# Gate and up matrices of a mixture of experts tiled by input chunks, with a wait and a release for each half

## The reference

```python
def expert_choice_ffn(h, w_router, w_gate, w_up, w_down):
    b, n, d = h.shape
    cap = max(1, (EC_CAPACITY * n) // N_EXPERTS)
    aff = jax.nn.softmax((h @ w_router).astype(jnp.float32), axis=-1)
    g, idx = lax.top_k(jnp.swapaxes(aff, 1, 2), cap)
    xe = jax.vmap(lambda hb, ib: hb[ib])(h, idx)
    a = jnp.einsum('becd,edf->becf', xe, w_gate)
    up = jnp.einsum('becd,edf->becf', xe, w_up)
    y = jnp.einsum('becf,efd->becd', jax.nn.silu(a) * up, w_down) * g[..., None].astype(h.dtype)
    return jax.vmap(lambda ib, yb: jnp.zeros((n, d), h.dtype).at[ib.reshape(-1)].add(yb.reshape(-1, d)))(idx, y)
```

## Time and profile before

| | |
|---|---|
| median of 3 runs | 2900.12 us (2898.72 to 2900.56) |
| profiled execution, span from first to last instruction | 2896.6 us |
| PE busy | 2609.4 us (90%) |
| DVE busy | 1336.6 us (46%) |
| ACT busy | 961.9 us (33%) |
| POOL busy | 39.3 us (1%) |
| bytes moved | 796.13 MB, mean 275 GB/s |
| mean granted clock of PE | 0.968 of full |
| chain that ended last | PE 72%, DMA 19%, DVE 4%, ACT 3%, issue 2% |

### The profile page before, as it was taken

The page is one execution under the profiler, slowest core; times in us unless marked ns, Lnnn a source line. Parts: engine busy times, 40 slices in busy tenths (PEclk is TensorE's granted clock), DMA queues, the critical chain, the costliest instruction groups (busy, mean ns, idle before and its releaser), DMA issues.

```text
span 2896.6 us, 34037 instructions
## 1 busy us (share of the span) xinstructions
PE 2609.4 (90%) x13004; PEld 1714.1 (59%) x13004; DVE 1336.6 (46%) x2308; ACT 961.9 (33%) x1782; POOL 39.3 (1%) x51
## 2 busy tenths in 40 slices
PE   8999878787889888877779899999999999999999
PEld 3436423222465543222245789878988988985787
DVE  1764300001266520000025687567887458865676
ACT  3124210101121320000013555556555446544443
POOL 0010000000000000000000000000000000000000
PEclk9999999999999999999999999989999999999999
DMA  8674499999945459999991486515866427852242
GB/s 362 278 306 192 203 428 429 428 429 429 428 193 224 168 231 429 428 428 429 428 394 63 164 340 251 236 59 217 322 263 256 172 113 269 343 212 88 83 178 102
DMA packets 59492, 796.13 MB, mean 275 GB/s; under 512 B 8636, under 2 KB 9916, under 8 KB 10748
## 3 DMA queue, kind: packets, MB, share of 16 engines
q1 hardware_dynamic: 55664, 790.13, 66.8%
q10 hardware_dynamic: 3724, 4.59, 0.5%
HBM read 793.64 MB, written 1.05 MB: 274 GB/s over the span
## 4 chain that ended last, share of the span: by engine, by line
PE 72%; DMA 19%; DVE 4%; ACT 3%; issue 2%; SPq 0%; ACTq 0%; DVEq 0%; POOL 0%; POOLq 0%
PE banks L2008 12%; PE banks L2032 9%; PE banks L1504 8%; DMA ring<-in_t_gate 7%; PE banks L925 6%; DMA ring<-in_t_up 6%; PE banks L810 5%; PE banks L940 5%; DMA ring<-in_t_down 4%; PE banks L1520 3%; DMA arena<-in_t_gate 3%; PE banks L2025 2%; PE banks L1379 2%; PE banks L1573 2%; PE banks L797 2%
## 5 line engine op out<-in xcount | busy, mean ns | idle before, releaser
L1504 PE MATMUL banks<-ring,arena 128*64 128x512 f32 x1920 | 475.3, 619 | 100.9 <-DMA ring<-in_t_up 54.8
L1504 PEld LDWEIGHTS banks<-ring,arena 128*64 128x64 f32 x1920 | 162.3, 143 | 389.1 <-issue 345.4
L2633 DVE TENSOR_TENSOR arena<-arena,banks 128x512 f32<-128x512 f32 x32 | 22.0, 687 | 795.2 <-PE banks L1504 795.2
L3096 DVE TENSOR_TENSOR ring_lo<-ring,w_hi 128x1024 fp32r<-128x1024 f32 x256 | 313.3, 1225 | 133.9 <-ACT w_hi L2427 131.7
L2427 ACT CAST w_hi<-ring 128x1024 fp32r<-128x1024 f32 x256 | 268.4, 1055 | 314.9 <-PE banks L2008 166.3
L2032 PE MATMUL banks<-u_pair,w_hi 128*128 128x256 f32 x1536 | 278.8, 284 | 3.9 <-DVE ring_lo L3096 3.3
L2140 ACT COPY arena<-banks 32x512 f32 x96 | 55.3, 576 | 608.3 <-PE banks L1520 607.5
L2032 PEld LDWEIGHTS banks<-u_pair,w_hi 128*128 128x128 f32 x1536 | 240.1, 192 | 6.7 <-issue 3.9
L1520 PE MATMUL banks<-ring,arena 128*64 128x512 f32 x896 | 206.9, 616 | 28.4 <-DMA ring<-in_t_down 15.7
L2032 PE MATMUL banks<-u_pair,ring_lo 128*128 128x256 f32 x768 | 217.3, 283 | 0.0
L2008 PE MATMUL banks<-w_hi,ffn_h_hi 128*128 128x512 f32 x512 | 200.9, 392 | 0.0
(11 more groups left out here) (391 smaller groups left out, 4098.8 us busy)
## 6 DMA issues: line engine op xcount, KB each, us to landing
ring<-in_t_ffn SPq DMA_DIRECT2D x64, 2048.0 KB, 8.2
ring<-in_t_gate SPq DMA_DIRECT2D x60, 2048.0 KB, 22.0
ring<-in_t_up SPq DMA_DIRECT2D x60, 2048.0 KB, 22.1
ring<-in_t_down SPq DMA_DIRECT2D x56, 2048.0 KB, 21.6
ring<-in_t_ada_dots SPq DMA_DIRECT2D x48, 2048.0 KB, 9.7
ring<-in_t_ada SPq DMA_DIRECT2D x24, 2048.0 KB, 17.1
ring<-in_t_ret_in SPq DMA_DIRECT2D x12, 2048.0 KB, 8.2
arena<-in_t_down SPq DMA_DIRECT2D x8, 2048.0 KB, 31.3
```

The source lines that it names most:

```text
L1504: mm = nc.tensor.matmul(PS[64 * h:64 * h + 64, f.bank, :], x_cur[:, b, k, :], wview(un[h0 + h], KC)[:, k, :], start=(k == 0), stop=(k == K ...
L3096: TT(w_lo, w, w_hi[:, n % 4].bitcast(F32), ALU.subtract).then_inc(S("ffn_w_lo"), 1)
```

## The change

- `weight_tiles` cuts gate and up with `rows(m, 4)`, as down already is: unit h now holds input chunks 4h to 4h+3 and all 1024 output columns.
- In `plan_moe`, the first unit of each matrix has a `used` mark of its own, on the semaphore `moe_half`; the second keeps the bank's `full` mark. There are three such marks in an expert, 12 in a round, 48 in a mixture.
- In the expert loop PE waits for a unit right before the first chunk that reads it, and the last matmul of chunk 3 of each matrix raises `moe_half`.
- The `selT` transposes become the function `turn_selw(lo)`, two token tiles at a call, each with its own wait on `moe_selw`. With two sequences the first two tiles are turned inside the gather, after the first half (`k0 == 0`) of the second sequence, and the last two after the gather. With one sequence both are turned after the gather, where they stood.

```diff
@@ weight_tiles
-        "t_gate": experts(w["w_gate"], columns),
-        "t_up": experts(w["w_up"], columns),
+        "t_gate": experts(w["w_gate"], lambda m: rows(m, 4)),
+        "t_up": experts(w["w_up"], lambda m: rows(m, 4)),
@@ plan_moe
-                for i, f in enumerate((g, g, u, u, d, d)):
-                    us[6 * j + i].used = f.full
+                for i, f in enumerate((g, u, d)):
+                    us[6 * j + 2 * i].used = Mark(S("moe_half"), 48 * l + 3 * j + i + 1, 12)
+                    us[6 * j + 2 * i + 1].used = f.full
@@ moe_pe, before the gather
+                def turn_selw(lo):
+
+                    for t in range(lo, lo + TC):
+                        f = plan[p + "selT"][t]
+                        pe.wait_ge(S("moe_selw"), 4 * l + t + 1)
+                        f.open(pe)
+                        w = moe_selw[:, t].rearrange("p e c -> p (e c)")
+                        for q in range(4):
+                            mm = nc.tensor.transpose(PS[:, f.bank, q * P:(q + 1) * P], w[:, q * P:(q + 1) * P], ident)
+                        mm.then_inc(f.full.sem, 1)
@@ moe_pe, in the loop over k0 of the gather and behind it
-
-                pe.wait_ge(S("moe_selw"), (4 if l else 0) + 2 * ns)
-                for t, f in enumerate(plan[p + "selT"]):
-                    f.open(pe)
-                    w = moe_selw[:, t].rearrange("p e c -> p (e c)")
-                    for q in range(4):
-                        mm = nc.tensor.transpose(PS[:, f.bank, q * P:(q + 1) * P], w[:, q * P:(q + 1) * P], ident)
-                    mm.then_inc(f.full.sem, 1)
+                        if s == 1 and k0 == 0:
+                            turn_selw(0)
+
+                turn_selw(2 * ns - TC)
@@ moe_pe, gate and up
-                            un[h0].landed.wait(pe, it)
-                            un[h0 + 1].landed.wait(pe, it)
                             for k in range(KC):
+                                u = un[h0 + k // 4]
+                                if k % 4 == 0:
+                                    u.landed.wait(pe, it)
                                 for h in range(2):
                                     mm = nc.tensor.matmul(PS[64 * h:64 * h + 64, f.bank, :], x_cur[:, b, k, :],
-                                                          wview(un[h0 + h], KC)[:, k, :], start=(k == 0),
+                                                          wview(u, 4)[:, k % 4, h * 512:(h + 1) * 512], start=(k == 0),
                                                           stop=(k == KC - 1), skip_group_check=True)
+                                if k == 3:
+                                    mm.then_inc(S("moe_half"), 1)
                             mm.then_inc(f.full.sem, 1)
@@ moe_pe, down
-                        un[4].landed.wait(pe, it)
-                        un[5].landed.wait(pe, it)
                         ft.free.wait(pe, it)
                         for fc in range(8):
+                            if fc % 4 == 0:
+                                un[4 + fc // 4].landed.wait(pe, it)
                             for h in range(2):
...
+                            if fc == 3:
+                                mm.then_inc(S("moe_half"), 1)
                         mm.then_inc(fd.full.sem, 1)
```

## The result

The changed kernel takes 2884.45 us (median of 4 runs, 2884.28 to 2885.0) against 2900.28 us before: the ratio is 0.9949, with a 95% interval of 0.9935 to 0.9963. The profiled execution has a span of 2883.0 us against 2896.6.

The account below looks back on a forecast made before the run. Both mixtures were taken as bound by transfers, with 5.8 us of slack an expert. Gains of 8.7 and 7.1 us, 15.8 off a 2896.6 us span, gave 2880.8; plus 3.5 to the median, 2884.3 us, range 2880 to 2892.

Parts of the forecast that it names:

- The first release: Start of each mixture: gate's first unit is released after 4 of 8 chunks, so transfers start 3.55 us earlier.
- The stream doesn't pause: Both mixtures: transfers run without gaps from first issue to last landing, 4.897 us a unit, with 3.8 and 3.9 us remaining.
- The end: Last down of each mixture: only its second half follows the last landing, gaining 4.8 us in mixture 0, 3.55 in mixture 1.
- The transposes: Selection transposes before mixture 0's experts: moved into the gather, they let PE start 0.3 us sooner; mixture 1 unchanged.
- The added waits: Middle of each matrix in the expert loops: a wait already over costs 0, at most 0.1 us.
- The clock: PE in the mixtures: a fall costs it 1.43 to 1.69 us, taken by slack; waits become 1.35 us, twice as many.
- The second rival: Both mixtures: falls of PE's clock at the waits make PE the bound, +108 us less the 15.8, 2992; chance 0.03.
- The gain passes through: Behind the mixtures: `combine` and later work move along with down, so the whole gain reaches the total.
- its own bound of 2 us: Stages other than the mixtures: a change above 2 us in any would refute that the gain passes through.
- The sum: Whole kernel: 8.7 us from mixture 0 and 7.1 from mixture 1, together 15.8 us off the span, to 2880.8.

Follow-up runs that it names:

- the early release alone: The changed kernel, but PE waits for both units of a matrix at its start, measured against the kernel before: 2893.57 us, ratio 0.998.
- The transposes alone: The kernel before with only the selection transposes moved into the gather: 2898.45 us, ratio 0.9999.
- the split waits alone: The changed kernel, but both units of a matrix are released at its end, measured against the kernel before: 2892.19 us, ratio 0.9978.

## Why the prediction was right, step by step

**The first release.** Forecast 3.55 us in each mixture; measured 3.44 (7.13 - 3.69, and 7.12 - 3.69 in mixture 1). A half isn't half of 7.09 but 3.65 us: sixteen records more cost 3.44 us (7.09 - 3.65), and 0.21 us stand once in each group, however long. Otherwise right, and the early release alone shows that the start is handed on.

**The stream doesn't pause.** From first issue to last landing 439.2 us in mixture 0 (439.6 before) and 430.0 in mixture 1 (429.9). Right.

**The end.** Forecast 4.8 and 3.55 us; measured 8.39 - 3.65 = 4.7 and 7.09 - 3.66 = 3.4. The first half of down was to fit by 0.3 us in mixture 0 and by 0.2 in mixture 1; it fits by 0.20 and 0.06. Right, but narrowly, and with a share of luck: 1.3 of the 4.7 us are what the low clock in the last up cost the kernel before in this one profile. The transposes alone, with up and down of before, met none there. In the changed kernel the last up ran in two groups of 3.65 us, without low clock.

**The transposes.** Forecast 0.3, measured 0.5 to 0.6. Two terms were 0.1 off: ACT's last copy moved from 316.14 to 317.07, 0.93 us rather than 1.04, and PE starts 0.23 us after POOL's first copy (317.63 + 0.61, by the earlier trace rows), not 0.35. The 0.55 us in the first row of the table of stages would not show this by itself: in the profiles of kernels with the same code up to the loop of mixture 0 that start lies anywhere from 317.15 to 321.25 us.

**The added waits** cost nothing: 64 records in 13.95 us as before. That half matrices from one unit run as fast as from two: right.

**The clock.** The second rival wanted more falls. There are fewer: over four experts of mixture 1 the granted clock is 0.99 where the earlier trace rows had 0.96, with waits about half as long. The experiments separate the cause: over the two loops the granted clock is 0.96 and 0.96 in the kernel before, 0.95 and 0.96 with the early release alone, which still waits for whole matrices, but 1.00 and 0.99 with the split waits alone and in the changed kernel. So here it is the splitting of the waits that keeps the clock up, and not the early release. The stretch of four experts in the changed kernel:

```profile
1185.00:1302.00 117.00, 91.13 (x400) 28.59 (x398) 5.52 (x8) 8.28 (x13) 1.61 (x4) 0.99 1.01 429
```

The advice of the Trainium skill ("TensorE: Matmul & The Clock Gate", "HAM oscillation — how this bites in real kernels") to thin-M kernels, to run all K-tiles before waiting for a DMA, does not hold for this stage: the waits inside the K loop replace longer ones outside of it.

**The gain passes through.** Here a step failed by its own bound of 2 us: between the mixtures the changed kernel takes 2.16 us more. The stretches behind `combine` and ahead of the second loop carry it, in the changed kernel

```profile
765.05:795.58 30.53, 25.59 (x154) 19.41 (x153) 11.52 (x23) 10.48 (x17) 2.68 (x1) 0.94 1.01 426
...
983.99:1047.49 63.50, 52.14 (x226) 40.41 (x226) 23.01 (x59) 21.21 (x41) 1.18 (x3) 0.89 0.35 133
```

and in the kernel before

```profile
774.12:803.17 29.05, 24.09 (x153) 18.76 (x153) 11.52 (x23) 10.48 (x17) 2.68 (x1) 1.00 0.98 414
...
992.61:1054.40 61.79, 50.37 (x227) 39.97 (x226) 23.07 (x59) 21.20 (x41) 1.24 (x3) 0.92 0.36 137
```

The same work takes 1.48 and 1.71 us longer at a granted clock of 0.94 and 0.89 instead of 1.00 and 0.92; between the two stretches the changed kernel is 1.03 us faster (188.41 against 189.44). No part of the change can be named as the cause: the moved transposes alone have 282.57 us between the mixtures and the early release 282.52, but the split waits, with the same moved transposes, have 279.91. The changed kernel has 282.44 and 282.41 in its two profiles. So where a fall of the clock lands differs from kernel to kernel by up to 2.7 us here, and seems to stay with a kernel; what sets it is open, and a prediction made from one profile can't know it.

**The sum.** The mixtures and the transposes were forecast at 15.8 us and gave 15.8 (8.52 + 6.74 + 0.55). The span fell by only 13.6, for the reason just given. That the median came out at the forecast, 2884.45 for 2884.3, has some luck in it: I had taken 3.5 us between span and median for a constant. It is about 2.0 us of what lies around the span (2883.0 and 2885.0 in the changed kernel's profiled execution, the same in each experiment) and about 1.5 us by which the profiled execution of before was shorter than the median. The changed kernel's profiled execution was 0.55 us longer than its median (2885.0 against 2884.45). So the errors, 2.2 us lost on the way against 1.5 and 0.55 us of offset, nearly cancel.

## What to carry to other kernels

Where a stage is bound by a stream of transfers, its length is the time to the first release, the stream, and the work behind the last landing. Cut both ends by the order in which data are used, and check first, by count times pace against first issue to last landing, that nothing pauses between; then check that the finer pieces keep the pace, which here 2 MiB pieces did and 1 MiB pieces didn't. At the start, check the second and third release too: a first issue made 1.7 us sooner was worth nothing 95 us later, in the version in which the issue behind it came as late as before.

When a gain is under 1%, compare lengths of stages between marks in the profile, and not only medians: the parts of this change add up to within 0.4 us that way, beside runs that scatter by several microseconds.

## What the runs showed of the hardware

Splitting each 2 MiB transfer (16 KiB a partition) into two of 1 MiB took the stream from 428 to 422 GB/s, 1.5%. In the version that splits 4 of 24, 2.2 us were lost within the first 95 us of the loop, and 0.08 us for each split unit after that.

The largest difference between profiles came from the stick-breaking attention block, far from the change. In the profile of the early release alone the stretch from the end of its projections to its last heads took 53.5 us, in the changed kernel 60.7. The rows (columns as in the earlier trace rows) are of about the same work, first in the changed kernel, then in the early release alone:

```profile
1890.30:1920.00 29.70, 28.19 (x108) 21.30 (x108) 21.01 (x43) 15.52 (x29) 0.00 (x0) 0.71 0.36 142
...
1920.00:1951.00 31.00, 28.92 (x157) 21.81 (x156) 27.22 (x54) 21.15 (x42) 0.00 (x0) 1.00 0.00 1
```

```profile
1897.50:1925.00 27.50, 25.43 (x133) 19.58 (x134) 24.75 (x52) 19.42 (x37) 0.00 (x0) 1.00 0.39 154
```

At a granted clock of 0.71, more than half of the time at 1.2 GHz, the first stretch gets through 108 PE records in 29.7 us; at 1.00 it is 133 in 27.5. The low level lasts for some 17 us there: between 1900 and 1910 us the granted clock is 0.50 although PE is busy without a gap, and from 1910 to 1920 it is 0.98. This one stretch is worth 7 us, almost half of what the change gained. Such a low stretch is the rule: from the last projection matmul to the next group of the same line (L926) the block takes 54.3 to 54.5 us in seven of the ten profiles and 56.2 and 56.3 in two more, and only the early release alone, at a granted clock of 1.00, has 47.2. Its profiled execution took 2885.18 us where the median of that kernel is 2893.57. What decides it was not tried.
